# Sample attention: four neighbouring tokens of a cache page in one SBUF partition

## The reference, cut to what matters

```python
ka_all = concatenate([gather_pages(cache_k_a, l, page_table), ka_s], axis=1)   # 1024 past + 8 new tokens
oa_s = dsa_attend(qa_s, ..., ka_all, va_all, ...)             # branch A: softmax over kept keys
ob_s = stick_breaking_attend(qb_s, pos_s, kb_all, vb_all, ..) # branch B: reverse cumulative sums
```

## Time and profile before

| | |
|---|---|
| median of 3 runs | 2334.97 us (2334.24 to 2339.71) |
| profiled execution, its own time | 2330.57 us |
| span of its trace | 2328.8 us |
| mean granted TensorE clock | 0.967 of full speed |
| PE busy in the whole span | 2137.2 us, 92% |
| DVE, ACT busy | 1380.7 us (59%), 761.7 us (33%) |
| bytes moved by DMA | 218.91 MB, mean 94 GB/s |

### The profile page before, as it was taken

The page is one execution under the profiler, slowest core; times in us unless marked ns, Lnnn a source line. Parts: engine busy times, 40 slices in busy tenths (PEclk is TensorE's granted clock), DMA queues, the critical chain, the costliest instruction groups (busy, mean ns, idle before and its releaser), DMA issues. The chain is left out here.

```text
span 2328.8 us, 36216 instructions
## 1 busy us (share of the span) xinstructions
PE 2137.2 (92%) x13337; PEld 1763.6 (76%) x13337; DVE 1380.7 (59%) x2404; ACT 761.7 (33%) x1430; POOL 110.2 (5%) x120
## 2 busy tenths in 40 slices
PE   6878999999998988987886989799999999999995
PEld 6636888888875565565555878699999999999994
DVE  6378787456665655764444543356665666656656
ACT  4172101121118876763334331221222212222122
POOL 0000000000005550001000000000000000000000
PEclk9899999999999999998998999899999999999997
DMA  4411223222224105615997340111101111011102
GB/s 165 121 39 67 86 82 122 86 82 85 85 69 102 41 10 127 217 56 177 365 359 259 136 145 1 50 49 33 54 27 54 50 31 54 27 54 52 30 22 91
DMA packets 186065, 218.91 MB, mean 94 GB/s; under 512 B 28828, under 2 KB 119324, under 8 KB 184796
## 3 DMA queue, kind: packets, MB, share of 16 engines
q1 hardware_dynamic: 179588, 214.96, 28.2%
q10 hardware_dynamic: 6360, 2.38, 0.4%
HBM read 181.17 MB, written 36.13 MB: 93 GB/s over the span
## 5 line engine op out<-in xcount | busy, mean ns | idle before, releaser
L2673 DVE TENSOR_TENSOR x_all<-x_all,ff_down 128x512 f32<-128x512 f32 x396 | 269.9, 688 | 159.4 <-PE ff_down L2577 159.3
L2562 PE MATMUL ff_up<-m_hi,ff_up_hi 128*128 128x368 f32 x1056 | 348.3, 330 | 7.5 <-DVE ff_up_lo L2650 7.5
L2563 PE MATMUL ff_up<-m_lo,ff_up_hi 128*128 128x368 f32 x1056 | 349.1, 331 | 0.0
L2564 PE MATMUL ff_up<-m_hi,ff_up_lo 128*128 128x368 f32 x1056 | 347.3, 329 | 0.0
L558 PE MATMUL pr_acc<-pr_w_hi,h_hi 128*128 128x512 f32 x720 | 282.8, 393 | 8.0 <-PEq L838 8.0
L559 PE MATMUL pr_acc<-pr_w_lo,h_hi 128*128 128x512 f32 x720 | 282.5, 392 | 0.0
L560 PE MATMUL pr_acc<-pr_w_hi,h_lo 128*128 128x512 f32 x720 | 282.5, 392 | 0.0
L990 DVE TENSOR_SCALAR_CACHE_REDUCE bi_flags<-scores,bi_thr 128x384 bf16<-128x384 f32 (+6 forms) x231 | 215.9, 993 | 1.2
L2562 PEld LDWEIGHTS ff_up<-m_hi,ff_up_hi 128*128 128x128 f32 x1056 | 198.8, 188 | 8.7 <-DVE ff_up_lo L2650 7.9
L2563 PEld LDWEIGHTS ff_up<-m_lo,ff_up_hi 128*128 128x128 f32 x1056 | 198.8, 188 | 0.8
L2564 PEld LDWEIGHTS ff_up<-m_hi,ff_up_lo 128*128 128x128 f32 x1056 | 198.9, 188 | 0.0
(11 more groups left out here) (270 smaller groups left out, 3580.0 us busy)
## 6 DMA issues: line engine op xcount, KB each, us to landing
out_proj<-pr_staged SPq DMA_DIRECT2D x90, 256.0 KB, 2.0
up_raw<-in_w_up SPq DMA_DIRECT2D x44, 512.0 KB, 5.0
w_raw<-in_w_in SPq DMA_DIRECT2D x10, 2048.0 KB, 8.5
sa_keys<-in_cache_k_a SPq DMA_DIRECT2D x64, 256.0 KB, 4.1
sa_values<-in_cache_v_a SPq DMA_DIRECT2D x64, 256.0 KB, 7.5
sa_keys<-in_cache_k_b SPq DMA_DIRECT2D x64, 256.0 KB, 6.4
sa_values<-in_cache_v_b SPq DMA_DIRECT2D x64, 256.0 KB, 5.3
ff_down_raw<-in_w_down SPq DMA_DIRECT2D x22, 512.0 KB, 3.5
```

Of the source, the lines that this page charges most:

```text
L2562: pe.matmul(up[n][:], w, hi[:, c, at], start=c == 0, stop=False)
L2563: pe.matmul(up[n][:], w, lo[:, c, at], start=False, stop=False)
L2564: ins = pe.matmul(up[n][:], w_rest, hi[:, c, at], start=False, stop=c == KC - 1)
L2673: dve.tensor_tensor(at, at, down[n][:], ALU.add).then_inc(down_added.sem, 1)
```

## The change

A page now lies on 32 partitions, with four neighbouring tokens one after the other in each: 32 rows of 8 KB. Four pages stand side by side in the four bands of 32 partitions and fill four slots. The sizes of all tiles, the number of DMAs and of every other instruction, the waits and the orders of all queues stay.

- `load_half`: page j goes to band j % 4 and to slots 4 (j // 4) to 4 (j // 4) + 3. Slot 4 g + r then holds, in partition 32 b + q, token 4 q + r of page 4 g + b.
- `empty_page`: the transposed slot holds every fourth token of four pages. It is written to `keys_t` with a step of four elements (16 bytes), so that `keys_t` and the scores are in the order of tokens as before.
- `turn_probs`: the transposes read every fourth column of the 512 probabilities of a group, so that `prob_t` is in the order of the values' slots.

```diff
-    RING = 3
+    RING, RUN = 3, 4
+    BAND = P // RUN
...
     def load_half(self, sp, h, numbers, to, cache, sem):
         for j, n in enumerate(numbers):
-            sp.dma_start(to[h % self.RING][:, j, :], cache[bass.ds(n, 1), :, :]
-                         .rearrange("a p d -> p (a d)")).then_inc(sem[h % self.RING], 16)
+            group, band = divmod(j, self.RUN)
+            sp.dma_start(to[h % self.RING][band * self.BAND:(band + 1) * self.BAND, group * self.RUN:(group + 1) * self.RUN, :]
+                         .rearrange("q r d -> q (r d)"), cache[bass.ds(n, 1), :, :]
+                         .rearrange("a (q r) d -> q (a r d)", r=self.RUN)).then_inc(sem[h % self.RING], 16)
...
                     for j in range(4):
-                        ins = pe.transpose(turned[k][:, cols(j)], prob[b][:, cols(4 * k + j)], ident[:])
+                        of = prob[b][:, 512 * k:512 * (k + 1)].rearrange("p (n r) -> p n r", r=loads.RUN)[:, :, j]
+                        ins = pe.transpose(turned[k][:, cols(j)], of, ident[:])
...
-            copy(keys_t[c][:, :, cols(j % 4)], turned[g % 2][:].rearrange("p (a n) -> p a n", a=PAIRS)
+            in_order = keys_t[c][:].rearrange("p a (b q r) -> p a b q r", q=loads.BAND, r=loads.RUN)[:, :, :, :, j % loads.RUN]
+            copy(in_order, turned[g % 2][:].rearrange("p (a b q) -> p a b q", a=PAIRS, q=loads.BAND)
                  ).then_inc(emptied[g % 2], 1)
```

## The result

The changed kernel takes 2418.24 us (2413.25 to 2422.07, four runs) against 2334.60 us of the kernel before beside it: a ratio of 1.0351, 95% interval 1.0329 to 1.0372, 83.6 us slower. The direction was forecast, the size was not: 2356 was predicted, and the time lies 10 us above the range. Of the cases laid out ahead it is the rival "the loads become the bound". The profiled execution took 2419.15 us, with a span of 2417.4.

A forecast was written before the change was run, and what follows sets the result against it. In the sample stage PE's chain (21.4 us a unit) and the transfers (21.7) were taken as nearly balanced. Copies +23.5, probabilities +3.4 and waits -6.4 gave +20.5 us on 2330.57, 2351.1; with 4.4 for the median, 2356, range 2328 to 2408.

The forecast's parts named there:

- the loads become the bound: Rival, sample stage: loads bind below 310 GB/s; at 238 GB/s +73 us, 2408; chance 0.16 beyond the forecast's +10 to +45.
- The loads: Page loads of the sample stage: 8 KB rows move at 387 to 417 GB/s, ends 238 and 417; at most 7.6 us gained.
- The row of the masks: 16 mask loads, each to 8 partitions: 119 GB/s, half the engines busy; read as 476 GB/s for 32 partitions or 238 by engine.
- The copies: Key copies with a step of four, on DVE and ACT: 48 steps each 0.49 us longer, +23.5 us.
- The scan's 2.08 ns an element: DVE's slowest rate in the sample stage, taken as the high end for its stepped copy: 1.215 us.
- twice ACT's slope: ACT's stepped copy: its slope of 0.84 ns an element doubled, giving a copy of 1.02 us.
- the 1.83 forecast: PE's step for a pair of key pages: 0.49 us more, 1.83 us, with DVE's copy deciding.
- The probabilities: 64 transposes of the probabilities loading weights with a step of 16 bytes, in the open on PE: +3.4 us, ends 0 and 6.7.
- What goes back: PE's four waits for loads vanish, as a longer unit of 24.7 us needs only 340 GB/s: -6.4 us.
- What would show it: Signs in the profile after; prediction wrong if copies keep their length, PE waits for DMA every unit, or slices stay under 310 GB/s.

The follow-up runs named there:

- Run 7: Loads only against the kernel before: a page on 64 neighbouring partitions, rows of 4 KB, pages alternating between the halves; 1.0274, 66.1 us slower.
- run 4: Loads only against the kernel before: pages on 32 neighbouring partitions as in the change, but rows of 2 KB; 1.0389, 89.6 us slower.
- run 2: Only the loads of the change (32 neighbouring partitions, rows of 8 KB) against the kernel before, copies and transposes as before; 1.0364, 85.2 us slower.
- run 3: Loads only against the kernel before: rows of 8 KB, a page on every fourth of the 128 partitions; 1.0063, 14.8 us slower.
- run 5: Only the loads of the change against the kernel before, bands in the order 0, 2, 1, 3, so pages alternate between the halves; 1.0281, 66.5 us slower.
- run 6: Loads only against the kernel before: 8 KB rows, a page on every second partition of one half of 64; 1.0344, 83 us slower.
- run 1: Only the copies of the keys written with a step of four against the kernel before, loads and probabilities as before; 1.0063, 14.3 us slower.
- run 9: Only the transposes of the probabilities read with a step of four columns against the kernel before, loads and copies as before; 0.9999, no change.
- run 8: Only the values' pages on 32 neighbouring partitions against the kernel before, keys' pages on all 128, copies and transposes as before; 1.0353, about 76 us slower.

## Why the prediction was wrong, point by point

**The loads: the step that failed.** "I take 387 to 417, because rows of 8 KB are nearer to the weights' 4 KB than to the masks' 2 KB, and the bytes per partition that the mask row allows are ample." The row of the masks had two readings: a rate per partition (476 GB/s for 32) and a rate per engine (238). The first was used, the second kept as an end of the range. Run 7 decides against the first: twice the partitions give 237 GB/s and not 462, so it is no rate per partition. Row length, by which the choice was made, has next to no part in it: 218 and 223 GB/s for rows of 2 and 8 KB on neighbouring partitions (runs 4 and 2), and above 400 for the same 8 KB on others (run 3). The size was at hand in the masks: 119 GB/s on eight engines are 14.9 each, and 231 on 16 are 14.4. That both have one cause is not shown, so the agreement may be luck; a rate per engine it is not, since the same engines run above 400 in run 3. What decides is which partitions a page lies on: any layout inside one half of 64 was slow (the change, runs 2 and 4 to 7).

**The rival, sized.** Its sum has one half load too many. Six of the 32 half loads are issued while `sparse` runs, and a seventh before 1078.49; before (first line) and after (the others) the queue reads

```profile
1069.09 4.78 SPq L1756 DMA_DIRECT2D sa_keys<-in_cache_k_b  x8
...
1081.32 4.20 SPq L1758 DMA_DIRECT2D sa_keys<-in_cache_k_b  x8
1090.13 13.23 SPq L1758 DMA_DIRECT2D sa_keys<-in_cache_k_a  x16
```

So 25 are left, 52.4 MB and not 54.5. At 238 GB/s they would have given +64 us instead of +73, an upper end of 2399 instead of 2408, and loads that bind below 298 instead of 310. At the measured 231 they take 227 us: 1078.5 + 227 + 10 = 1315.5, 71 us behind the 1244.4 of before. The queue also gets to this point 11.6 us later (1090.13 for 1078.49), which the sum left out, and that makes 83. Measured were 83.6 in the median and 88.6 in the profiled execution. With 26 half loads and no later start the sum would give 80, close to the mark because the two slips nearly cancel: luck. The rival's arguments against itself both fell. The mask loads were no faster for each engine, and that "the pages of the other bands follow at once in the queue" helps little: even with the halves in turn run 5 gains 11%.

The Trainium skill (SBUF — State Buffer, Door 1: The DMA port swizzle) has partitions 0 to 31 and 0 to 63 on the same 8 of 16 ports, and about 218 GB/s as their limit. Runs 4 and 6, with 218 and 221, agree; run 2 and the change, with 223 and 231, lie 2 and 6% above it, and run 7, whose pages alternate between the halves, 9%. The prediction said that the page has nothing on a stream that changes between the bands. It has no such stream, but what bears on it was passed over: the part "Can I just issue two DMAs to hit both halves?" states that two DMAs to the two halves together gained 6% over one. Runs 5 and 7 show 11% and 6% over the 223 of run 2.

**The copies.** Predicted 1.215 us for DVE and 1.02 for ACT; both took 1.085, so ACT's copy, not DVE's, now frees the buffer that PE waits for (0.72 us in the pair). The scan's 2.08 ns an element was too slow a model for DVE (1.085 us makes 1.83 ns behind the same fixed part of 150 ns), and twice ACT's slope too quick for ACT. With the measured 1.085 DVE's own step would be 1.70 us; that the 1.83 forecast from it meets the 1.82 that ACT's copy sets is luck. Alone, run 1, they cost 14.3 us; by the steps it would have been 23.5 - 6.4 = 17.1. In the change itself they cost nothing, behind the loads.

**The probabilities.** 3.4 us taken, 0.7 us on PE and nothing measurable in the time (run 9). The term took the longer loads to lie in the open.

**What goes back.** "PE's four waits vanish" held only with the old loads (1.05 us left in run 1); with the new ones they became ten waits of 50.0 us.

**What would show it.** The line "if the slices stay under 310 GB/s with all engines busy" named the outcome.

## What to carry to other kernels

Between 2 and 8 KB it was not the row length but which partitions were reached that set a DMA's rate here: before a tile is laid on fewer partitions, look for any transfer in the trace that already lands on few, and read its GB/s beside the engines' busy share. With full engines at a low rate, more transfers in the queue helped little here, even to other partitions (11% in run 5). When a row has two readings that lie far apart, and the only difference between them is what the limit is counted by, neither similarity of size nor of shape chooses between them, and both deserve a chance of their own.

## What the runs showed of the hardware

- Pages of 256 KB that lie inside one half of 64 partitions moved at 218 to 231 GB/s with all engines busy (the change, runs 2, 4 and 6), at 237 and 247 with the halves in turn (runs 7 and 5); on every fourth of the 128 partitions slices reached 429 (run 3).
- Wide transfers are slower beside narrow ones: 2 KB packets 124 ns for 84 on the median (run 8).
- SP's issue of a page depends on its layout: 0.32 us at least for 32 neighbouring partitions, 0.33 for all 128, and 0.47 for every second or fourth partition and for 64 neighbours in rows of 4 KB alike.
- A copy of 512 elements from PSUM with a step of 16 bytes on its output takes 1.085 us on DVE (0.690 contiguous) and on ACT (0.595) alike.
- A transpose that writes PSUM with a step of 16 or 8 bytes takes PE no longer (median 273 ns in both kernels), and a weight load with that step 212 ns instead of 140, nearly all of it hidden.
